# Norms between stages in column parts, a native gate matrix, and a stacked first product in the product-key loop

## What is computed

```python
def rms_norm(x, gain):
    y = xf * lax.rsqrt(jnp.mean(xf * xf, axis=-1, keepdims=True) + EPS)
...
        h = rms_norm(x, norm_mix[l]) * (1.0 + scale_m) + shift_m
        x = x + gate_m * hybrid_mixer(h, ...)
        h = rms_norm(x, norm_ffn[l]) * (1.0 + scale_f) + shift_f
        x = x + gate_f * hierarchical_moe(h, ...)
...
    sv, si = lax.top_k(s, PEER_TOPK)
    ...
    gate = jax.nn.softmax(cv, axis=-1)
        act = jax.nn.gelu(jnp.einsum('cd,ced->ce', xc, u_tab[ec]))
        return jnp.einsum('ce,ced->cd', act * gc, v_tab[ec])
...
        x = _layer_norm(ALPHA * x + mix, ln1_g[l], ln1_b[l])
        x = _layer_norm(ALPHA * x + _peer(...), ln2_g[l], ln2_b[l])
```

## Time and profile before

| | |
|---|---|
| median of 3 runs | 3546.12 us (3544.0 to 3546.68) |
| profiled execution | 3544.96 us, its span 3543.2 us |
| TensorE matmul busy | 3237.9 us, 91% |
| VectorE, ScalarE, GpSimd busy | 62%, 42%, 5% |
| chain that ended last | TensorE 79%, VectorE 12%, DMA 3%, ScalarE 3% |
| granted TensorE clock, mean over the span | 0.95 of full |

### The profile page before, as it was taken

The page is one execution under the profiler, slowest core; times in us unless marked ns, Lnnn a source line. Parts: engine busy times, 40 slices in busy tenths (PEclk is TensorE's granted clock), DMA queues, the critical chain, the costliest instruction groups (busy, mean ns, idle before and its releaser), DMA issues.

```text
span 3543.2 us, 49865 instructions
## 1 busy us (share of the span) xinstructions
PE 3237.9 (91%) x17336; PEld 2783.4 (79%) x17336; DVE 2198.4 (62%) x4328; ACT 1495.8 (42%) x2377; POOL 163.2 (5%) x297
## 2 busy tenths in 40 slices
PE   3987999898899997799899999998689989999997
PEld 2667888667788876688789999987578978999996
DVE  3636777452677737198966666654538986666664
ACT  1314666332566624117734444432411953444442
POOL 1110000010000000041000000000004000000000
PEclk9987999898899998899999999999799999999998
DMA  5644888471688841242355555543034146555552
GB/s 200 246 148 178 291 296 297 151 256 56 227 296 299 298 156 59 68 143 78 94 194 188 188 185 185 187 154 140 30 103 137 66 131 193 186 185 189 188 185 89
DMA packets 166716, 614.78 MB, mean 174 GB/s; under 512 B 18704, under 2 KB 18736, under 8 KB 165536
## 3 DMA queue, kind: packets, MB, share of 16 engines
q1 hardware_dynamic: 151200, 551.62, 45.9%
q0 software_dynamic: 15360, 61.16, 5.0%
HBM read 611.66 MB, written 1.05 MB: 173 GB/s over the span
## 4 chain that ended last, share of the span: by engine, by line
PE 79%; DVE 12%; DMA 3%; ACT 3%; DVEq 2%; issue 1%; POOL 0%; ACTq 0%; POOLq 0%
PE PS L1460 18%; PE PS L1461 18%; PE PS L1462 18%; PE PS L1485 7%; PE PS L1927 4%; DMA arena<-in_w_ada 3%; PE PS L1948 2%; PE PS L1497 2%; PE PS L1947 1%; DVE arena L847 1%; PE PS L1507 1%; DVE arena L1331 1%; DVE arena L1332 1%; DVE arena L1338 1%; PE PS L1687 1%
## 5 line engine op out<-in xcount | busy, mean ns | idle before, releaser
L875 DVE TENSOR_TENSOR w_lo<-arena,w_hi 128x1024 fp32r<-128x1024 f32 x448 | 530.2, 1220 | 1.9 <-ACT w_hi L511 1.9
L511 ACT ACTIVATE w_hi<-arena 128x1024 fp32r<-128x1024 f32 x448 | 452.0, 1054 | 120.6 <-DMA arena<-in_v_t 76.9
L1462 PE MATMUL PS<-x_hi,w_lo 128*128 128x256 f32 x1536 | 435.1, 283 | 0.0
L1461 PE MATMUL PS<-x_lo,w_hi 128*128 128x256 f32 x1536 | 435.0, 283 | 0.0
L1460 PE MATMUL PS<-x_hi,w_hi 128*128 128x256 f32 x1536 | 434.1, 283 | 0.0
L1460 PE MATMUL PS<-w_hi,pw_hi 128*128 128x512 f32 x1024 | 404.4, 395 | 19.2 <-DVE w_lo L875 19.2
L1461 PE MATMUL PS<-w_lo,pw_hi 128*128 128x512 f32 x1024 | 403.0, 394 | 0.0
L1462 PE MATMUL PS<-w_hi,pw_lo 128*128 128x512 f32 x1024 | 400.6, 391 | 0.0
L818 ACT ACTIVATE arena<-PS 128x256 f32<-128x256 f32 x192 | 73.9, 385 | 638.1 <-PE PS L1462 638.1
L1435 DVE TENSOR_TENSOR arena<-arena 128x256 f32<-128x256 f32 x192 | 81.8, 426 | 392.2 <-ACT arena L818 392.2
L1102 DVE TENSOR_TENSOR gu_lo<-raw,gu_hi 128x1024 fp32r<-128x1024 f32 x256 | 297.5, 1221 | 29.1 <-ACT gu_hi L602 28.7
(11 more groups left out here) (417 smaller groups left out, 5786.2 us busy)
## 6 DMA issues: line engine op xcount, KB each, us to landing
raw<-in_w_gu SPq DMA_DIRECT2D x256, 512.0 KB, 5.3
arena<-in_u_t SPq DMA_DIRECT2D x256, 512.0 KB, 4.4
arena<-in_v_t SPq DMA_DIRECT2D x256, 512.0 KB, 3.5
arena<-in_w SPq DMA_DIRECT2D x152, 512.0 KB, 3.5
raw<-in_w_down SPq DMA_DIRECT2D x128, 512.0 KB, 5.4
arena<-in_w_ada POOLq DMA_DIRECT2D x96, 512.0 KB, 5.1
arena<-in_tab POOLq DMA_DIRECT2D x2, 1664.0 KB, 14.7
arena<-in_x POOLq DMA_DIRECT2D x2, 1632.0 KB, 8.7
```

Source lines behind the costliest of these rows:

```text
L511: A(w_hi[:, m % RING], ring[:, m % RING], ACT.Copy).then_inc(S["hi_done"], 1)
L875: V.tensor_tensor(w_lo[:, m % RING], ring[:, m % RING], w_hi[:, m % RING].bitcast(F32), ALU.subtract)\
L1461: mm(dst, w[0], m[1], start=False, stop=False)
L1462: return mm(dst, w[1], m[0], start=False, stop=stop)
```

## The change

Four things change.

- Norms in parts. x is squared in four parts of two chunks (`norm_sq` counts parts), and TensorE sums each as it comes (`squares`); for mix to moe these sums, and for nsa to peer the sums of the mean (`means`), stand between the output pairs. The eight scalings on VectorE are one chunk each (`scaled`), gain and shift move to ScalarE, chunk by chunk (`chunk_ok`), and the next stage's first matmuls wait for their chunk. The evacuation at the end of moe is in four parts (`x_part`), released by the scatter's matmuls in four parts. At the end of peer the copies, the transposes' release and the addition are in parts, the sum of `x_hi` and `x_lo` waits for the last first product in place of the transposes, and the output leaves in four loads of two chunks.
- In mix 0 the sixteen products with w_ada are spread 5, 5, 6 over the first three evacuations, and the column sums use bank 5; `ada_mod(1, ...)` stands in moe behind the norm.
- The gate matrix is made by one native float32 matmul a token; `OA_lo`, the ratio and its reciprocal go.
- `up` in the loop: `x_lo` and `x_hi` stand one behind the other as `x_lh`; per chunk one matmul of 512 columns (`w_hi` with both) and one of 256 (`w_lo` with `x_hi`, added onto the second half). ScalarE copies the first half (`up_lo`), VectorE adds the second (`up_sum`), ScalarE applies the gelu.

The diff, cut to its core:

```diff
-        NORM = {s: i for i, s in enumerate([s for s in plan if s[0] in ("mix", "moe")])}
+        def wait_x(eng, s, k):
+            kind, l = plan[SIDX[s] - 1]
+            if kind == "moe":
+                eng.wait_ge(S["x_part"], 4 * l + k // 2 + 1)
+            else:
+                eng.wait_ge(S["chunk_ok"], KT * (SIDX[s] - 1) + k + 1)
...
+            def root(s, rs, bank, eps):
+                act.wait_ge(S["norm_ss"], SIDX[s] + 1)
+                A(rs, PS[:, bank, 0:T], ACT.Ln, scale=1.0 / D, bias=eps)
+            def norm(s, sq, rs, q):
+                kind, l = s
+                for j in range(4):
+                    if kind == "moe":
+                        act.wait_ge(S["pair_evac"], PAIR["mix", l] + 8 + j + 1)
+                    elif SIDX[s]:
+                        act.wait_ge(S["x_part"], 4 * (l - 1) + j + 1)
+                    else:
+                        act.wait_ge(S["x_load"], 16)
+                    A(sq[:, 2 * j:2 * j + 2], x[:, 2 * j:2 * j + 2], ACT.Square).then_inc(S["norm_sq"], 1)
+                root(s, rs, 7, EPS)
+                for k in range(KT):
+                    act.wait_ge(S["scaled"], KT * SIDX[s] + k + 1)
+                    A(h[:, k], h[:, k], ACT.Identity, scale=gas[:, l, q, k:k + 1], bias=mods[:, l, 24 * q + k:24 * q + k + 1])\
+                        .then_inc(S["chunk_ok"], 1)
...
+                s = ("peer" if q else "nsa", l)
+                for j in range(4):
+                    act.wait_ge(S["ln_c"], 4 * LN[s] + j + 1)
+                    A(L_["sq"][:, 2 * j:2 * j + 2], x[:, 2 * j:2 * j + 2], ACT.Square).then_inc(S["norm_sq"], 1)
+                root(s, L_["rs"], LN_BANK[q] + 1, LN_EPS)
+                for k in range(KT):
+                    act.wait_ge(S["scaled"], KT * SIDX[s] + k + 1)
+                    A(x[:, k], x[:, k], ACT.Identity, scale=c2(l, f"ln{q + 1}_g", k, 1), bias=c2(l, f"ln{q + 1}_b", k, 1))\
+                        .then_inc(S["chunk_ok"], 1)
+                act.drain().then_inc(S["x_ready"], 1)
...
-                A(gh_hi[:], PS[:, 1, 0:T], ACT.Copy).then_inc(S["pk_tev"], 1)
+                A(gT, PS[:, 1, 0:T], ACT.Copy)
-                act.wait_ge(S["pk_gr"], l + 1)
-                    for i in range(4 * g, 4 * g + 4):
-                        act.wait_ge(S["pt_a"], T * l + i + 1)
-                        if i >= GDEEP:
-                            act.wait_ge(S["pt_mm"], T * l + i - GDEEP + 1)
-                        A(OA_lo[:, i % GDEEP], OA_hi[:, i % GDEEP].bitcast(F32), ACT.Identity, scale=grT[:, i:i + 1]).then_inc(S["pt_lo"], 1)
...
-                        A(pb[:, j % 2], PS[:, 4 + j, 0:T], ACT.Gelu_apprx_tanh).then_inc(S["gelu_ok"], 1)
+                        A(pb[:, j % 2], PS[:, 4 + j, 0:T], ACT.Copy).then_inc(S["up_lo"], 1)
+                        act.wait_ge(S["up_sum"], (PK - EARLY) * l + PEER_STEP * i + j + 1)
+                        A(pb[:, j % 2], pb[:, j % 2], ACT.Gelu_apprx_tanh).then_inc(S["gelu_ok"], 1)
-                A(L_["y"].rearrange("p a (b c) -> p (a b) c", c=512), PS[:, 0:4, :], ACT.Copy).then_inc(S["y2_ev"], 1)
+                for q in range(2):
+                    for t in range(TT):
+                        last = A(L_["y"][:, t, 512 * q:512 * q + 512], PS[:, 2 * t + q, :], ACT.Copy)
+                    last.then_inc(S["y2_ev"], 1)
...
-                    if l == 0:
-                        ada(1, 4 * j, 4 * j + 4)
+                    if l == 0 and j < 3:
+                        ada(1, (0, 5, 10)[j], (5, 10, 16)[j])
+                dve.drain().then_inc(S["x_ready"], 1)
+            def moe(l):
+                norm(("moe", l), E["rs"])
-                    ada_mod(1, 0, 2, 6)
-                dve.drain().then_inc(S["x_ready"], 1)
-            def moe(l):
-                norm(("moe", l), E["rs"], 1)
+                    ada_mod(1, 0, 2, 5)
-                dve.wait_ge(S["rt_pe"], 10 * l + RT_PE["logits"])
+                dve.wait_ge(S["rt_pe"], RT_N * l + RT_PE["logits"])
...
-                dve.wait_ge(S["rt_pe"], 10 * l + RT_PE["out"])
+                for j in range(4):
+                    dve.wait_ge(S["rt_pe"], RT_N * l + RT_PE["out"] + j)
+                    for k in (2 * j, 2 * j + 1):
+                        last = V.scalar_tensor_tensor(x[:, k], PS[:, j, T * (k % 2):T * (k % 2) + T],
+                                                      mods[:, l, 40 + k:41 + k], x[:, k], ALU.mult, ALU.add)
+                    last.then_inc(S["x_part"], 1)
+                dve.drain().then_inc(S["x_ready"], 1)
+            def layer_norm(l, q):
+                s = ("peer" if q else "nsa", l)
+                dve.wait_ge(S["ln_mu"], LN[s] + 1)
+                for j in range(4):
+                    V.scalar_tensor_tensor(x[:, 2 * j:2 * j + 2], PS[:, LN_BANK[q], 0:T].unsqueeze(1).to_broadcast([P, 2, T]), -1.0 / D,
+                                           x[:, 2 * j:2 * j + 2], ALU.mult, ALU.add).then_inc(S["ln_c"], 1)
+                dve.wait_ge(S["norm_rs"], SIDX[s] + 1)
-                    last = V.scalar_tensor_tensor(x[:, k], PS[:, k // 2, T * (k % 2):T * (k % 2) + T],
-                                                  mods[:, l, 40 + k:41 + k], x[:, k], ALU.mult, ALU.add)
-                last.then_inc(S["x_ready"], 1)
-            def layer_norm(l, q):
-                n = LN["peer" if q else "nsa", l]
-                dve.wait_ge(S["ln_mu"], n + 1)
-                V.scalar_tensor_tensor(x[:], PS[:, 6, 0:T].unsqueeze(1).to_broadcast([P, KT, T]), -1.0 / D, x[:],
-                                       ALU.mult, ALU.add).then_inc(S["ln_c"], 1)
-                dve.wait_ge(S["ln_rs"], n + 1)
-                V.tensor_tensor(x[:], x[:], L_["rs"].unsqueeze(1).to_broadcast([P, KT, T]), ALU.mult)
-                dve.drain()
-                for k in range(KT):
-                    last = V.tensor_scalar(x[:, k], x[:, k], c2(l, f"ln{q + 1}_g", k, 1), c2(l, f"ln{q + 1}_b", k, 1), ALU.mult, ALU.add)
-                last.then_inc(S["x_ready"], 1)
+                    V.tensor_tensor(x[:, k], x[:, k], L_["rs"], ALU.mult).then_inc(S["scaled"], 1)
...
-                dve.wait_ge(S["pk_tev"], 2 * l + 1)
-                g_hi = gh_hi[:].bitcast(F32)
-                V.tensor_scalar(grT, g_hi, 1e-30, None, ALU.max)
-                V.tensor_tensor(OB_f, PS[:, 1, 0:T], g_hi, ALU.subtract)
-                dve.drain()
-                V.reciprocal(grT, grT)
-                dve.drain()
-                V.tensor_tensor(grT, grT, OB_f, ALU.mult).then_inc(S["pk_gr"], 1)
-                dve.wait_ge(S["pk_tev"], 2 * l + 2)
-                dve.drain()
+                dve.wait_ge(S["pk_tev"], l + 1)
-                    V.tensor_scalar(OA_hi[:, i % GDEEP], cc("iota"), ebT[:, 0, i:i + 1], g_hi[:, i:i + 1], ALU.is_equal, ALU.mult)\
+                    V.tensor_scalar(OA[:, i % GDEEP], cc("iota"), ebT[:, 0, i:i + 1], gT[:, i:i + 1], ALU.is_equal, ALU.mult)\
...
+                        f = pb[:, j % 2]
+                        dve.wait_ge(S["up_lo"], (PK - EARLY) * l + PEER_STEP * i + j + 1)
+                        V.tensor_tensor(f, f, PS[:, 4 + j, T:2 * T], ALU.add).then_inc(S["up_sum"], 1)
-                        f = pb[:, j % 2]
-                dve.wait_ge(S["y2t"], l + 1)
+                dve.wait_ge(S["slot_done"], BASE_SPLIT["peer", l] + PEER_SLOTS - 1)
-                V.scalar_tensor_tensor(x[:], x[:], ALPHA, PS[:, 4:8, :].rearrange("p a (b c) -> p (a b) c", c=T), ALU.mult, ALU.add)\
-                    .then_inc(S["z2_ok"], 1)
+                for j in range(4):
+                    dve.wait_ge(S["y2t"], 4 * l + j + 1)
+                    V.scalar_tensor_tensor(x[:, 2 * j:2 * j + 2], x[:, 2 * j:2 * j + 2], ALPHA,
+                                           PS[:, 4 + j, :].rearrange("p (b c) -> p b c", c=T), ALU.mult, ALU.add).then_inc(S["z2_ok"], 1)
+                dve.drain()
...
+            def squares(s, sq, j, bank=7):
+                pe.wait_ge(S["norm_sq"], 4 * SIDX[s] + j + 1)
+                for k in (2 * j, 2 * j + 1):
+                    last = mm(PS[:, bank, 0:T], ones, sq[:, k], start=k == 0, stop=k == KT - 1)
+                if j == 3:
+                    last.then_inc(S["norm_ss"], 1)
+            def pairs(n0, p0, n, rhs, ready=None):
...
+                            if ready and j + q == 0:
+                                wait_x(pe, ready, k)
...
-                for _ in pairs(n0 + W1_IN, p0 + 8, 4, M["mixT"]):
-                    pass
+                for j in pairs(n0 + W1_IN, p0 + 8, 4, M["mixT"]):
+                    if j:
+                        squares(("moe", l), E["sq"], j - 1)
+                squares(("moe", l), E["sq"], 3)
-                    ada_cols(1, 0, 2, 6)
+                    ada_cols(1, 0, 2, 5)
...
+                    if k % 2:
+                        last.then_inc(S["rt_pe"], 1)
+            def means(l, q, j):
+                s = ("peer" if q else "nsa", l)
+                if q:
```

(42 more changed lines are left out.)

112 lines of the change are left out of this document (36 added, 76 removed).

## The result

The changed kernel takes 3439.0 us (median of 4 runs, 3431.6 to 3440.8) against 3546.4 for the kernel before beside it: a ratio of 0.9692, 95% interval 0.9676 to 0.9707. The forecast was 3434, 3412 to 3464. The profiled execution took 3440.8, its span 3439.0, the clock 0.96 over the span.

What follows compares the result with a forecast made beforehand. TensorE, 79% of the chain that ended last, was taken as the bound. Norms 88.4, stacked product 17.7 and gate matrix 5 sum to 111.1 us off 3544.96, giving 3434, range 3412 to 3464.

Steps and rivals of the forecast that it cites:

- Norms: At the stage boundaries: norms handed on in parts let TensorE start earlier, 88.4 us less in sum.
- All eight terms: Norm savings: nsa-peer 19.5, peer 0-nsa 1 16.1, peer 1-end 17.6, mix 1-moe 1 6.1, moe 0-mix 1 8.7, moe 1-nsa 0 3.3, mix 0-moe 0 13.1, mix 0 start 4.1.
- moe 0 to mix 1: Boundary after moe 0: 17.8 us becomes 9.1 (eight matmuls 6.0, root 2.2, front 0.95), saving 8.7.
- mix 0 to moe 0: Boundary after mix 0: 23.3 us from the last product with w_ada becomes 10.2, saving 13.1.
- The rival of half clock in more of the pieces: Between stages: paired matmuls with gaps keep TensorE at 1.2 GHz, 20 us lost, about 3454; 13%.
- the higher clock: Router and head of gate matrix: shorter waits leave TensorE at 2.4 GHz, some 15 us less, 3419; 10%.
- Stacked product: First product in the loop: two 256-column matmuls become one of 512, 0.0115 us less per chunk, 17.7 us, range 0 to 17.7.
- I take the dense 0.228: Stacked product in the loop: a 512-column matmul with a two-piece operand was assumed to take the dense rate, 0.228 us.
- the loop keeps its time: Product-key loop: the two-piece operand or extra waits eat the 17.7 us, about 3450; 12%.
- Gate matrix: Gate matrix in both layers: without the ratio and reciprocal its start is 2.5 us shorter each, 5 us.
- VectorE stays the bound, without gaps: Gate matrix: VectorE's 0.92 us per two tokens exceeds TensorE's 0.88, one-hot pairs run without gaps, so the stretch keeps 117 us.
- turn to TensorE: Gate matrix: TensorE at 0.95 us per pair of tokens becomes the bound, both layers lose 8 us, 3442; 8%.

Runs made afterwards that it cites:

- e11: Changed kernel, but the next stage's first matmul waits for all eight gain-and-shift pieces, not its own: 3456.8 us, ratio 0.9745.
- e4: Kernel before with only the norms in parts; loop and gate matrix as before: 3450.2 us, ratio 0.9720.
- e7: Changed kernel without the loop's 256-column matmuls (w_lo with x_hi), the copy and the sum: 3231.8 us.
- e9: Changed kernel with the stacked first product reordered, eight 512-column matmuls first, then eight of 256: 3416.3 us, ratio 0.9636.
- e12: Changed kernel with each chunk's second matmul widened to 512 columns, so weights alternate but width never changes: 3581.4 us.
- e5: Changed kernel with x_lo and x_hi of a chunk side by side, the moving operand one piece of 512 columns: 3434.4 us, ratio 0.9676.
- e2: Changed kernel with stacked matmuls kept, but ScalarE's copy and VectorE's sum left out, gelu reading the second half directly: 3437.1 us, ratio 0.9689.
- e8: Changed kernel with ScalarE's 128 x 128 product per token put back in the gate matrix, into an unread buffer: 3435.9 us, ratio 0.9681.
- e10: Changed kernel with the stacked first product in pairs, two matmuls of 512 columns, then two of 256: 3418.1 us.
- e6: Changed kernel whose loops load and split only the first 128 of 1024 weight columns, matmuls the same: 3431.5 us.

## Why the forecast was right, and where it was not

- **Norms, 88.4 forecast, 92 found.** All eight terms hold to 1.5 us. The largest misses are moe 0 to mix 1 (1.4) and mix 0 to moe 0 (1.3). In the first I took 6.0 us for the eight sums at mostly half clock; they took 4.8. In the second the part that I had counted, from the last evacuation to the router, came out as counted (252.97 - 242.83 = 10.1, forecast 10.2), so the 1.3 lies ahead of it, and why stays open. The rival of half clock in more of the pieces shows in no stretch as a loss, and the higher clock didn't give 15 us; some 5 us in the gate stretches are of its kind (below), 1.7 of them perhaps by chance, and mix 1 lost 3.3. e11 shows the front's mechanism; the other steps (sums moved ahead, parts under one another) stand on the timelines and on the sum of them all in e4.
- **Stacked product, 17.7 forecast, 2.4 found.** The step that failed is "I take the dense 0.228" with 0.120 beside it: each rate was right for a run of its own width (0.2267 in e7, e9, e12), but the kernel sets a narrow matmul between two wide ones, and that costs 8 x 0.0125 = 0.10 us a pass, more than the 0.092 to be saved. The pass gained 0.027 because the order before carried 0.02 of the same kind. The term's lower end, nothing, and the rival "the loop keeps its time" (12%) held it, but the rival's total of 3450 didn't come, since norms and gate matrix gave 11 us more than forecast; and of the causes that I gave there, the two-piece operand costs nothing (e5). I had counted the copy and the sum at nothing. In the steady pass that is so (e2); at the ends of the loop there is no cover, 1.5 us a layer. Of the missing 15.3 us the pass thus accounts for 192 x 0.065 = 12.5 and the ends for 3.
 The Trainium skill's figure ("TensorE: Matmul & The Clock Gate", "Wait — 56ns, not 53.3ns?"), about 2.5 ns a matmul, gave 4 us and came nearest. The runs don't bear it out as the reason: at one width the fixed part is 2 x 0.120 - 0.2267 = 13 ns, and e9 gets the 15 us.
- **Gate matrix, 5 forecast, 12 found.** The start is as forecast: from ScalarE's copy to the first one-hot row 0.9 us, 3.5 before, 2 x 2.55. The step "VectorE stays the bound, without gaps" was wrong for before: I had divided 117.3 us by 255 without looking for waits, and counted TensorE's 0.88 at full clock only. At half clock it held VectorE up, 1.7 and 1.8 us in the two layers; the one-hot rows gained 4.0. A further 1.7 can't be laid to the change: ahead of the gates of peer 0 the same sixteen records of early blocks (eight native matmuls) ran at half clock before and at full clock after, but they ran at half clock, 5.41 us, in 10 of the 24 such places in after and its variants too, e8 among them:

```profile
1608.49 5.41 PE L1927 MATMUL PS<-x,arena 128*128 128x256 f32 x16 [3.41 <-ACT arena L778]
```
```profile
1563.96 3.72 PE L1940 MATMUL PS<-x,arena 128*128 128x256 f32 x16 [2.28 <-ACT arena L800]
```

 The last 1.4 stands behind the last one-hot row, where VectorE waits for what ScalarE still has to copy: 2.8 us before and 2.1 after in peer 1, and 2.3 in e8, which has ScalarE's products back. 5.1 + 4.0 + 1.7 + 1.4 = 12.2. The stretch didn't turn to TensorE.
- **Stage bodies, 0 forecast, 2.7 lost**, 3.3 of it in mix 1. The granted clock there fell from 0.95 to 0.93. By my estimate a hundredth costs 1.35 us of 135, since a hundredth of mean clock is 2% of the time at half clock, so this would be 2.7 of the 3.3:

```profile
697.00:830.00 133.00, 127.35 (x582) 91.98 (x581) 67.42 (x76) 47.26 (x49) 15.90 (x29) 0.95 0.61 210
```
```profile
668.00:804.00 136.00, 129.76 (x581) 93.29 (x580) 69.20 (x80) 50.25 (x56) 15.47 (x29) 0.93 0.61 209
```

Why it fell more often, no run tests.

Cutting on VectorE costs about what the forecast took from the earlier trace rows: four parts take 2.48 us and one whole 2.29, eight pieces 2.77, and all but the first stand beside ScalarE's pieces.

## What to carry to other kernels

A norm between stages costs TensorE its whole chain of whole-tile steps; hand it on by chunk, on two engines in turn, and let the next stage wait for its own chunk: here 92 us of 3546. When matmuls of two widths are mixed, put like beside like, at least in pairs, and measure the mix, since rates taken from runs of one width need not add up in another order. Before a pace is called an engine's own, look for waits inside it and for the granted clock of the stretch. A step that is hidden in every pass of a loop is not hidden in its first and its last.

## What the runs showed of the hardware

- In fp32r with a new weight tile for each matmul, 512 columns take 0.2267 us from start to start, 28 or 20 in a row to the nanosecond, and 256 columns 0.120. A single 256 between two of 512 costs 12.5 ns more (after, 5.593 us a pass against a sum of 5.494); with two of each a pass is only 0.013 us over that sum (e10).
- The slowing isn't where its cause is: in after the second product, all of 512, took 2.783 us in place of 12 x 0.2267 = 2.720 (e7, e12), though only the first product mixes widths.
- After 4.68 us without a matmul TensorE ran at 1.2 GHz, 0.50 of full, for some 7 us (before and e4, both layers); after 1.63 us without one it stayed at 2.4 GHz (after and eleven variants, both layers). After 1.8 to 2.3 us without one it went either way: the same sixteen records took 3.72 or 5.41 us.
- Loads at 188 or at 24 GB/s, and the splits of VectorE and ScalarE at full or an eighth, leave TensorE's pass at 5.593 us both times (after, e6).
